# Three quarters of a second feed-forward matrix by seven block products, in a hybrid decoder layer

## The reference

```python
    u = rmsnorm(h, norm_mlp[i])
    h = h + jnp.square(jax.nn.relu(u @ w_ff1[i])) @ w_ff2[i]
    gate = jax.nn.sigmoid(rmsnorm(h, norm_ple[i]) @ w_ple_gate[i])
    h = h + gate * (p[i] @ w_ple_proj[i])
```

## Time and profile before

| | us |
|---|---|
| median of 3 runs | 2656.12 (2655.86 to 2659.14) |
| the profiled execution's own time | 2664.68 |
| its span | 2663.1 |
| TensorE busy | 2567.0 (96%) |
| VectorE, ScalarE, GpSimd busy | 1510.1, 1275.8, 535.1 |
| first feed-forward matrix | from 1092.5 to 1743.2 |
| second feed-forward matrix | from 1743.2 to 2444.8 |

### The profile page before, as it was taken

The page is one execution under the profiler, slowest core; times in us unless marked ns, Lnnn a source line. Parts: engine busy times, 40 slices in busy tenths (PEclk is TensorE's granted clock), DMA queues, the critical chain, the costliest instruction groups (busy, mean ns, idle before and its releaser), DMA issues.

```text
span 2663.1 us, 49051 instructions
## 1 busy us (share of the span) xinstructions
PE 2567.0 (96%) x18322; PEld 2105.7 (79%) x18322; DVE 1510.1 (57%) x2008; ACT 1275.8 (48%) x1721; POOL 535.1 (20%) x381
## 2 busy tenths in 40 slices
...
GB/s 203 155 152 156 139 138 157 162 156 159 152 131 99 123 95 134 119 127 134 127 133 134 134 130 130 138 238 121 119 118 122 122 118 118 98 99 101 97 98 106
DMA packets 503741, 352.26 MB, mean 132 GB/s; under 512 B 57173, under 2 KB 468807, under 8 KB 502663
## 3 DMA queue, kind: packets, MB, share of 16 engines
...
## 4 chain that ended last, share of the span: by engine, by line
PE 58%; issue 28%; DVE 6%; ACT 4%; DMA 2%; POOL 1%; SPq 1%; DVEq 0%; ACTq 0%; POOLq 0%
PE bank L1244 15%; PE acc L733 7%; PE bank L1245 7%; PE acc L735 7%; PE acc L734 7%; PE acc L1140 2%; PE acc L1142 2%; PE acc L1141 2%; ACT w_hi L1341 1%; POOL sumsq L2610 1%; PE bank L921 1%; PE acc L931 1%; PE bank L931 1%; DVE pr L2029 1%; PE bank L941 1%
## 5 line engine op out<-in xcount | busy, mean ns | idle before, releaser
L1898 DVE TENSOR_TENSOR w_lo<-w_raw,w_hi 128x1024 fp32r<-128x1024 f32 x292 | 359.5, 1231 | 680.3 <-ACT w_hi L1341 678.3
L1341 ACT ACTIVATE w_hi<-w_raw 128x1024 fp32r<-128x1024 f32 x292 | 308.9, 1058 | 783.1 <-PE acc L735 728.5
L1244 PE MATMUL bank<-mix,w_hi 128*128 128x512 f32 x1568 | 569.0, 401 | 14.0 <-DVE tile_sums L2402 10.2
L1245 PE MATMUL bank<-mix,w_lo 128*128 128x256 f32 x1568 | 442.2, 282 | 0.0
L733 PE MATMUL acc<-hidden,w_hi 128*128 128x512 f32 x1024 | 399.1, 390 | 3.5 <-DVE w_lo L1898 3.5
L734 PE MATMUL acc<-hidden,w_hi 128*128 128x512 f32 x1024 | 399.1, 390 | 0.0
L735 PE MATMUL acc<-hidden,w_lo 128*128 128x512 f32 x1024 | 398.9, 390 | 0.0
L1244 PEld LDWEIGHTS bank<-mix,w_hi 128*128 128x128 f32 x1568 | 296.8, 189 | 90.2 <-issue 10.8
L733 PE MATMUL acc<-a_all,w_hi 128*128 128x512 f32 x800 | 320.5, 401 | 2.0 <-DVE w_lo L1898 2.0
L735 PE MATMUL acc<-a_all,w_lo 128*128 128x512 f32 x800 | 312.2, 390 | 0.0
L734 PE MATMUL acc<-a_all,w_hi 128*128 128x512 f32 x800 | 311.8, 390 | 0.0
...
## 6 DMA issues: line engine op xcount, KB each, us to landing
w_raw<-in_w_ff SPq DMA_DIRECT2D x128, 512.0 KB, 3.9
w_raw<-in_w_in SPq DMA_DIRECT2D x100, 512.0 KB, 3.9
parts<-in_w_ff SPq DMA_DIRECT2D x32, 1024.0 KB, 5.8
parts<-in_w_ff SPq DMA_DIRECT2D x64, 512.0 KB, 4.9
w_raw<-in_w_out SPq DMA_DIRECT2D x32, 512.0 KB, 4.0
hid_d<-sq ACTq DMA_DIRECT2D x32, 512.0 KB, 2.7
w_raw<-in_w_ple_gate SPq DMA_DIRECT2D x32, 512.0 KB, 3.9
...
```

Source lines behind the costliest of these rows:

```text
L1244: mm(dst[:, :], wh[:, j, :], mixed(x, j), start=fresh and j == 0, stop=False, skip_group_check=True)
L1245: last = mm(dst[:, 0:HT], wl[:, j, :], mixed(x, j)[:, 0:HT], start=False, stop=j == NJ, skip_group_check=True)
L1341: A(w_hi[:, s, :, :], w_raw[:, s ^ raw_turned[0], :, :], ACT.Copy).then_inc(sg("w_hi_ready"), 1)
L1898: V.tensor_tensor(w_lo[:, s, :, 0:width], w_raw[:, s ^ raw_turned[0], :, 0:width], w_hi[:, s, :, 0:width].bitcast(F32), ALU.subtract).then ...
```

## The change

Of the second matrix's 32 pairs of row tiles the first 24 (`RING`) are multiplied by seven products as well, in 24 steps, and the last eight as before (16 output tiles, one group). A step t takes output pair t mod 8 and the eight row pairs t to t+7 (mod 24). Their operands stay in `mix` and `mix_last`, where from step to step one row pair is exchanged for another. In eight steps each output pair has had eight row pairs, after 24 all of them.

While the first matrix runs, GpSimd also makes the sums S1 to S4 of each hidden pair (`sum_hidden`), and ScalarE's queue stores them to `hid_sums_d`. At the last pair of the first matrix SP fills the seven operands of the first eight row pairs (`fill`, two DMAs each), each when TensorE has used the old one for the last time; ScalarE copies (`fill_hi`), VectorE subtracts, for two of them GpSimd (`fill_lo`). In every step four DMAs bring the new row pair's operands (`refill`), ScalarE copies and VectorE subtracts them (`refill_hi`, `refill_lo`); TensorE waits for these before products 0, 2, 4 and 6 of the next step. A step's result is multiplied by `rstd` by GpSimd (`scale_rows`), added to the two rows of `h` that SP has loaded from `h_d` into `sumsq` and `tmp` (`add_rows`), and stored back (`store_rows`). The direct quarter's tiles then start from a freshly loaded `h2`, as before, with the fold of the norm beside them. Its first weights, for tile 1, are queued on SP behind the last `store_rows`.

The diff, cut to what the text speaks of; the common indent of 12 columns inside the engines' blocks is left away:

```diff
+    RING = 3 * PAIRS // 4
+    STEPS = PAIRS + RING
...
+    stream = sb("hidden", [P, KT, 2, T], [base + 32 * 1024], F32R)
+    g_hi_all = sb("g_hi_all", [P, KT, T], [base + 96 * 1024], F32R)
+    g_lo_all = sb("g_lo_all", [P, KT, T], [base + 128 * 1024], F32R)
+    hidden_sums = sb("hidden_sums", [P, 4, HT], [base + 162 * 1024])
+    row_pair_of = (sumsq, tmp)
...
+    FILL_TURN = (A11, A12, S2, S1, S3, S4, A22)
+    FILLS_OF_POOL = (2, 3)
+    BATCHES = ((A11, 2), (S1, 2), (S3, 2), (A22, 1))
+    FILLED = (64, 64, 64, 32)
...
+def load_second_parts(t, which):
+    p, m = PAIRS + t, t % UK
+    sums_made, turn = ((3, 1), (4, 5), (3, 5))[which]
+    sp.wait_ge(sg("weight_sums_made"), past("weight_sums_made") + 4 * (p - 1) + sums_made)
+    sp.wait_ge(sg("w_split"), FIRST + UNITS * (p - 1) + turn + 3)
+    for to, k0, n in ((m, t, UK - m), (0, (t + UK - m) % RING, m)) if m else ((0, t, UK // 2), (UK // 2, t + UK // 2, UK // 2)):
+        if which == 0:
+            sp.dma_start(parts[:, 0, to:to + n, :], ff2_parts[:, 0, k0:k0 + n, 2 * P * m:2 * P * (m + 1)]).then_inc(sg("part_landed0"), 16)
+        else:
+            sp.dma_start(parts[:, 1, to:to + n, (which - 1) * P:which * P],
+                         ff2_parts[:, 1, k0:k0 + n, 2 * P * m + (which - 1) * P:2 * P * m + which * P]).then_inc(sg(f"part_landed{which}"), 16)
+def hidden_block(u, k):
+    if u in (A11, A12):
+        return hid_d[k, :, u, 0:HT].rearrange("a p t -> p a t")
+    if u == A22:
+        return hid_d[k, :, 1, HT:T].rearrange("a p t -> p a t")
+    return hid_sums_d[k, :, u - S1, :].rearrange("a p t -> p a t")
+def fill(n):
+    u = FILL_TURN[n]
+    sp.wait_ge(sg("unit_done"), FIRST + 2 + UNITS * (PAIRS - 1) + n + 1)
+    if n >= 4:
+        sp.wait_ge(sg(f"refill_landed{n % 4}"), past(f"refill_landed{n % 4}") + 32)
+    sp.dma_start(ring_parts(u, slice(HT, T))[0].bitcast(F32), hidden_block(u, slice(0, NJ))).then_inc(sg(f"refill_landed{n % 4}"), 16)
+    sp.dma_start(mix_last[:, u:u + 1, HT:T].bitcast(F32), hidden_block(u, slice(NJ, UK))).then_inc(sg(f"refill_landed{n % 4}"), 16)
+def refill(t, b):
+    u, n = BATCHES[b]
+    k = (t + UK) % RING
+    if t == 0:
+        sp.wait_ge(sg(f"refill_landed{b}"), past(f"refill_landed{b}") + FILLED[b])
+    sp.wait_ge(sg("unit_done"), FIRST + 2 + UNITS * (PAIRS + t) + (2, 4, 6, 7)[b])
+    src = (hid_d[k, :, :, 0:HT], hid_sums_d[k, :, 0:2, :], hid_sums_d[k, :, 2:4, :], hid_d[k, :, 1:2, HT:T])[b]
+    sp.dma_start(ring(u, n, t % UK, slice(HT, T)).bitcast(F32), src).then_inc(sg(f"refill_landed{b}"), 16)
+def load_rows(t):
+    sp.wait_ge(sg("rows_moved"), past("rows_moved") + 64 * t)
+    for b in range(2):
+        sp.dma_start(row_pair_of[b][:, :], h_d[2 * (t % UK) + b]).then_inc(sg("rows_moved"), 16)
+def store_rows(t):
+    sp.wait_ge(sg("grown"), past("grown") + len(FILLS_OF_POOL) + 3 * (t + 1))
+    sp.wait_ge(sg("rows_moved"), past("rows_moved") + 64 * t + 32)
+    for b in range(2):
+        sp.dma_start(h_d[2 * (t % UK) + b], row_pair_of[b][:, :]).then_inc(sg("rows_moved"), 16)
+sp.wait_ge(sg("hidden_stored"), past("hidden_stored") + 16 * UK)
+sp.wait_ge(sg("sums_stored"), past("sums_stored") + 16 * UK)
+load_second_parts(0, 0)
+fill(0)
+load_second_parts(0, 2)
+load_second_parts(0, 1)
+fill(1)
+fill(2)
+fill(3)
+load_second_parts(1, 0)
+fill(4)
+fill(5)
+load_second_parts(1, 2)
+load_second_parts(1, 1)
+fill(6)
+load_rows(0)
+for t in range(RING):
+    if t < RING - 1:
+        if t == 0:
+            sp.wait_ge(sg("hidden_stored"), past("hidden_stored") + 16 * RING)
+            sp.wait_ge(sg("sums_stored"), past("sums_stored") + 16 * RING)
+        if t:
+            load_second_parts(t + 1, 0)
+        refill(t, 0)
+        if t:
+            load_second_parts(t + 1, 2)
+            load_second_parts(t + 1, 1)
+    if t:
+        store_rows(t - 1)
+    if t < RING - 1:
+        refill(t, 1)
+    if t:
+        load_rows(t)
+    if t < RING - 1:
+        refill(t, 2)
+        refill(t, 3)
...
+store_rows(RING - 1)
+second_units(0, 1)
+with sp.Fori(0, KT // 2 - 1) as i:
+    for b in range(2):
+        second_units(i, b, 1)
...
+        if p == PAIRS:
+            if u in FILLS_OF_POOL:
+                pe.wait_ge(sg("grown"), past("grown") + FILLS_OF_POOL.index(u) + 1)
+            else:
+                pe.wait_ge(sg("refilled"), past("refilled") + (1, 2, 0, 0, 3, 4, 5)[u])
+        elif p > PAIRS and u % 2 == 0:
+            pe.wait_ge(sg("refilled"), i * 4 + (past("refilled") + UNITS - len(FILLS_OF_POOL) + 4 * (p - PAIRS - 1) + u // 2 + 1))
...
+seven_products(0, PAIRS)
+with pe.Fori(0, RING - 1) as i:
+    seven_products(i, PAIRS + 1)
...
+def fill_hi(n):
+    u = FILL_TURN[n]
+    act.wait_ge(sg(f"refill_landed{n % 4}"), past(f"refill_landed{n % 4}") + (32 if n < 4 else 64))
+    for hi, src in zip(ring_parts(u, slice(0, HT)), ring_parts(u, slice(HT, T))):
+        last = A(hi, src.bitcast(F32), ACT.Copy)
+    last.then_inc(sg("refill_hi_ready"), 1)
+def refill_hi(i, t, b):
+    u, n = BATCHES[b]
+    act.wait_ge(sg(f"refill_landed{b}"), i * 16 + (past(f"refill_landed{b}") + FILLED[b] + 16 * (t + 1)))
+    turn = None if t % UK == NJ else i
+    A(ring(u, n, t % UK, slice(0, HT), turn), ring(u, n, t % UK, slice(HT, T), turn).bitcast(F32), ACT.Copy).then_inc(sg("refill_hi_ready"), 1)
+def second_his(i, t):
+    p = PAIRS + t
+    product_hi(i, p, 3)
+    product_hi(i, p, 0)
+    product_hi(i, p, 1)
+    refill_hi(i, t - 1, 1)
+    product_hi(i, p, 2)
+    refill_hi(i, t - 1, 2)
+    product_hi(i, p, 4)
+    refill_hi(i, t - 1, 3)
+    for u in range(5, UNITS):
+        product_hi(i, p, u)
+    if t < RING - 1:
+        refill_hi(i, t, 0)
+product_hi(0, PAIRS, 3)
+fill_hi(0)
+product_hi(0, PAIRS, 0)
+fill_hi(1)
+fill_hi(2)
+product_hi(0, PAIRS, 1)
+fill_hi(3)
+product_hi(0, PAIRS, 2)
+fill_hi(4)
+product_hi(0, PAIRS, 4)
+fill_hi(5)
+store_hidden(0, PAIRS - 1)
+product_hi(0, PAIRS, 5)
+fill_hi(6)
+product_hi(0, PAIRS, 6)
+refill_hi(0, 0, 0)
+for g in range(RING // UK):
+    if g:
+        second_his(0, g * UK)
+    with act.Fori(0, UK - 2) as i:
+        second_his(i, g * UK + 1)
+    second_his(0, g * UK + NJ)
...
+    if p > PAIRS:
+        dve.wait_ge(sg("grown"), i * 3 + (past("grown") + len(FILLS_OF_POOL) + 3 * (p - PAIRS) - 2))
...
+def fill_lo(n):
+    u = FILL_TURN[n]
+    dve.wait_ge(sg("refill_hi_ready"), past("refill_hi_ready") + n + 1)
+    for hi, lo in zip(ring_parts(u, slice(0, HT)), ring_parts(u, slice(HT, T))):
+        last = V.tensor_tensor(lo, lo.bitcast(F32), hi.bitcast(F32), ALU.subtract)
+    last.then_inc(sg("refilled"), 1)
+def refill_lo(i, t, b):
+    u, n = BATCHES[b]
+    dve.wait_ge(sg("refill_hi_ready"), i * 4 + (past("refill_hi_ready") + UNITS + 4 * t + b + 1))
+    hi, lo = (ring(u, n, t % UK, c, None if t % UK == NJ else i) for c in (slice(0, HT), slice(HT, T)))
+    V.tensor_tensor(lo, lo.bitcast(F32), hi.bitcast(F32), ALU.subtract).then_inc(sg("refilled"), 1)
+def second_pair(i, t):
+    p = PAIRS + t
+    product_lo(i, p, 3)
+    take_167(i, p - 1, 4)
+    sum_22(i, p - 1)
+    product_lo(i, p, 0)
+    sum_12(i, p - 1)
+    product_lo(i, p, 1)
+    refill_lo(i, t - 1, 1)
+    sum_21(i, p - 1)
+    product_lo(i, p, 2)
+    refill_lo(i, t - 1, 2)
+    take_first(i, p)
+    product_lo(i, p, 4)
+    refill_lo(i, t - 1, 3)
+    sum_11(i, p)
+    product_lo(i, p, 5)
+    take_16(i, p, 3, 2)
+    product_lo(i, p, 6)
+    take_fifth(i, p, 3)
+    if t < RING - 1:
+        refill_lo(i, t, 0)
+product_lo(0, PAIRS, 3)
+take_167(0, PAIRS - 1, 4)
+sum_22(0, PAIRS - 1)
+fill_lo(0)
+product_lo(0, PAIRS, 0)
+sum_12(0, PAIRS - 1)
+fill_lo(1)
+product_lo(0, PAIRS, 1)
+sum_21(0, PAIRS - 1)
+product_lo(0, PAIRS, 2)
+take_first(0, PAIRS)
+fill_lo(4)
+product_lo(0, PAIRS, 4)
+sum_11(0, PAIRS)
+fill_lo(5)
+product_lo(0, PAIRS, 5)
+take_16(0, PAIRS, 3, 2)
+fill_lo(6)
+product_lo(0, PAIRS, 6)
+take_fifth(0, PAIRS, 3)
+refill_lo(0, 0, 0)
+for g in range(RING // UK):
+    if g:
+        second_pair(0, g * UK)
+    with dve.Fori(0, UK - 2) as i:
+        end = chained(i, 3)
+        second_pair(i, g * UK + 1)
+    unchained(UK - 2, end)
+    second_pair(0, g * UK + NJ)
...
+def sum_hidden(i, k):
+    a11, a21, a12, a22 = sq[:, 0, 0:HT], sq[:, 0, HT:T], sq[:, 1, 0:HT], sq[:, 1, HT:T]
+    s1, s2, s3, s4 = (hidden_sums[:, n, :] for n in range(4))
+    made = past("hidden_sums_made") + 4 * k
+    pool.wait_ge(sg("hidden_squared"), i + (past("hidden_squared") + k + 1))
+    if k or not isinstance(i, int):
+        pool.wait_ge(sg("sums_stored"), i * 16 + (past("sums_stored") + 16 * k))
+    G.tensor_tensor(s1, a21, a22, ALU.add).then_inc(sg("hidden_sums_made"), 1)
+    G.tensor_tensor(s3, a11, a21, ALU.subtract).then_inc(sg("hidden_sums_made"), 1)
+    pool.wait_ge(sg("hidden_sums_made"), i * 4 + (made + 1))
+    G.tensor_tensor(s2, s1, a11, ALU.subtract).then_inc(sg("hidden_sums_made"), 1)
+    pool.wait_ge(sg("hidden_sums_made"), i * 4 + (made + 3))
```

(73 more changed lines are left out.)

132 lines of the change are left out of this document (55 added, 77 removed).

## The result

The change makes the kernel slower: 2702.11 us (median of 4 runs, 2700.71 to 2711.54) against 2657.63 (median of 4 runs beside them, 2655.86 to 2661.66). The ratio is 1.0159, with an interval of 1.0138 to 1.0181. The sign was as forecast and so was the mechanism of the steady steps; the size was not (+13.4 forecast, +44.5 between the medians), nor was the entry of the direct quarter. The time lies 0.1 us above the range of 2634 to 2702.

The account below looks back on a forecast made before the run. TensorE was taken to bound both matrices. Own work -47.0, step 0 +28, steady steps +30 and entry +2.4 gave +13.4 us on the median 2656.1: 2669.5 us, range 2634 to 2702 (forecast's own 2655 to 2684, chance 0.52).

Parts of the forecast that it names:

- the mechanism of the steady steps: Second matrix: refill splits wait out GpSimd's instructions, delaying the reduction ahead of product 2; +1.3 us a step, +30 in all.
- the entry of the direct quarter: Start of the last eight row pairs: the store of last rows delays tile 1's weights, +2.4 us (-3 to +6).
- 47.0 us: TensorE's own work: 521.9 us of tiles removed, 474.9 us of seven-product steps added, so -47.0 us.
- the hidden sums of the first matrix: First matrix: GpSimd's four half-width sums a pair fit its idle time, cost 0; at most 3 us a pair uncovered.
- Rival A: Steady steps: refill splits mostly miss GpSimd's fourth sum; step 20.1 us, total -15, 2641 us; chance 0.27.
- the lock: VectorE instructions with two SBUF inputs and GpSimd ones reading SBUF exclude each other for a whole instruction; steps cost +30 us.
- C (transfers): Rival: transfers bind in every step, landings up to 11.2 us instead of 5; P 22.5, +62, 2701 us; chance 0.08.
- P = 21.3: Length in us of a steady step of the second matrix as worked out; 21.1 was taken, bounds 19.79 and 22.5.
- rival B: Steady steps: each step's stall also drops TensorE's clock; +18 us, 2687 us; chance 0.13.
- step 0: Second matrix's first step: filling all seven operands stalls TensorE; sum 30 us, 28 taken, bounds 17 and 36.
- the step to the median: The profiled execution lay 0.3% above its median; the same +13.4 us was put on the median 2656.1, giving 2669.5.
- The sum of all ends: Whole kernel: all terms' bounds added together, -33 to +57 us around the forecast of +13.4.

Follow-up runs that it names:

- Experiments 2 to 4: Each on the changed kernel: GpSimd's multiplication by rstd cut to 64 tokens, 2651.61 us; row stores cut to 16 of 128 partitions, 2711.23; refill splits reading PSUM, 2666.59.
- Experiment 5: Changed kernel with SP's load of the last rows behind four staged loads and tile 0's weights, 2696.33 us; with their store also behind tile 1's weights, 2693.59.
- experiment 4: Changed kernel with VectorE's refill splits reading an extra ScalarE copy in PSUM: 2666.59 us, 1.0007 of the kernel before.
- experiment 8: Changed kernel with PSUM refill splits, entry reorder and fills first; on top, GpSimd's fourth weight sum for step 0 waits for VectorE's first fill split: 2644.4 us (0.9945).

## Why the prediction was right, and where it failed

**Right:** that TensorE bounds both matrices and gives back 47.0 us; that the hidden sums of the first matrix cost nothing (19.75 us a pair); that the added splits, SBUF-only, wait out GpSimd's instructions, that this shows ahead of product 2 and hardly elsewhere; that the transfers don't bind. Experiments 2 to 4 show the cause and its size: all of the steps' 35.8 us go when one operand is read from PSUM, with the same work on GpSimd and the same transfers. The rule that the prediction weighed (the Trainium skill, page "SBUF — State Buffer", section "Who interferes with whom": two SBUF inputs on VectorE and a GpSimd instruction exclude each other) is borne out by them: 0.62 us a split with one input in PSUM, 1.51 with both in SBUF. Rival A (the lock mostly missed) falls, since 19 of 23 steps stall. C (transfers) falls as a mechanism; that its 2701 us lies next to the 2702 measured is chance.

**The failed step is the entry:** "Now SP's store of the last rows stands before tile 1's weights: the last hidden sum ends 4.4 us after the direct start", with "+2.4 (-3 to +6)". It measured +13.3, outside its own bounds. I followed SP's store ahead of tile 1's weights and overlooked SP's load of the last rows (2277.34) ahead of the staged loads: it waits for the store of step 22 to land (issued by 2274.99), so the staged loads come later, and with them VectorE's last hidden sum, at +11.6 instead of +4.4. GpSimd's work behind it was put at 5.2 us and took 7.8. What the runs showed in place of one idle time of 6.4 us ahead of tile 1 is two, 5.33 at the start and 7.48 ahead of tile 1. Experiment 5 changed both orders and gave back 14.0.

**Three terms were mis-sized.** First, the steps: the working gave P = 21.3 and I took "21.1, since some steps will meet GpSimd in a gap"; they took 21.35. No row stood behind that reduction, and it cost 4.6 of the 5.8 us missed. Part of the 21.35 is rival B's mechanism, which I had priced as a case of its own instead of inside the step: half a clock, here after six of the 19 idle times. TensorE was busy 465.9 us there and 452.8 in experiment 4, on the same instructions: 13 of the 35.8 us are slower matmuls, the other 23 idle time. Six falls of the clock at 1.6 us make about 10 of the 13; the remaining 3 are open. That 21.3 came so near the measured mean is therefore partly luck: it was laid out without the clock. Second, step 0: 34.8 for 28. The lock also takes in the fill splits (in experiment 8 the idle time at the start fell from 6.73 to 4.08 us without one of those waits), and A22's split sits ahead of product 5's reduction in VectorE's list; the forecast's bound of 36 held. Third, the step to the median: "I put the same difference on the median" carried a difference of two single executions over; the kernel before's lay 7.0 above its median and the changed kernel's 1.4 below. Of the 31 us by which the difference was missed, 10.9 are the entry, 6.8 step 0, 5.8 the steps, 8.5 this, and -1.0 the rest.

The sum of all ends, -33 to +57, held the result; the range that I drew from it stopped at +46. The errors of the terms all had one sign, and two of them were mine alone: 28 taken where the working gave 30, and 21.1 where it gave 21.3.
